# The opening of a three-layer transformer kernel: first modulation in pieces of 256 columns

## The reference, cut to what matters

```
c_act = silu(c)                                    # 1024 values
mod = c_act @ ada_w[0] + ada_b[0]                  # 1024 x 6144
sh1, sc1, g1, sh2, sc2, g2 = split(mod, 6)
h = rms_norm(x, norm_g[0, 0]) * (1 + sc1) + sh1
z = gelu(h @ a_w_in); u, v = split(z, 2)           # 1024 x 2048
v = layer_norm(v, a_ln_g, a_ln_b)
mixed = einsum(tril(a_w_s), v) + a_b_s             # per group of 128 channels, over 128 tokens
y = (u * mixed) @ a_w_out
x = x + g1 * rms_norm(y, norm_g[0, 1])
```

## Time and profile before

| | us |
|---|---|
| median of 3 runs | 1553.88 |
| the runs | 1557.81, 1553.88, 1552.71 |
| span of the profiled execution | 1551.4 |
| TensorE busy in it | 1507.1 (97%) |
| DVE / ACT / POOL busy | 1095.7 / 692.6 / 286.1 |
| chain that ended last, on TensorE | 81% |

### The profile page before, as it was taken

One profiled execution on the slowest core, in us unless ns is written; L12 is line 12 of the kernel. 1 busy time (PEld: TensorE's weight loads), 2 busy tenths in 40 slices (PEclk: granted clock), 3 DMA queues, 4 the chain that ended last, 5 costly groups with the idle time before them and its releaser, 6 DMA issues.

```text
span 1551.4 us, 20894 instructions
## 1 busy us (share of the span) xinstructions
PE 1507.1 (97%) x8187; PEld 1252.2 (81%) x8187; DVE 1095.7 (71%) x1607; ACT 692.6 (45%) x1177; POOL 286.1 (18%) x230
## 2 busy tenths in 40 slices
PE   4999999999999999989999999999999999999998
PEld 3888888888888897977788988888888988677677
DVE  6798688889989764269885785556634824799775
ACT  3433551322214544357774642313233525887651
POOL 0200013223232000058870020111100011010210
PEclk9999999999999999999999999999999999999999
DMA  9675257578584315230001164443332232211101
GB/s 332 243 265 181 82 204 246 189 248 293 184 294 161 107 34 174 77 108 2 2 2 56 56 225 160 159 144 115 132 109 83 84 109 66 92 61 55 55 1 55
DMA packets 108808, 203.35 MB, mean 131 GB/s; under 512 B 6041, under 2 KB 13478, under 8 KB 108710
## 3 DMA queue, kind: packets, MB, share of 16 engines
q1 hardware_dynamic: 108710, 202.01, 38.2%
HBM read 199.90 MB, written 2.10 MB: 130 GB/s over the span
## 4 chain that ended last, share of the span: by engine, by line
PE 81%; DVE 10%; issue 3%; DMA 2%; ACT 2%; POOL 1%; SPq 1%; DVEq 0%; POOLq 0%; ACTq 0%
PE PS L2142 47%; PE PS L2095 20%; DVE MACC L1287 3%; PE PS L2477 3%; PE PS L2504 2%; DVE WL L1253 2%; PE PS L2467 2%; PE PS L2654 1%; PE PS L2166 1%; DMA MRAW<-in_ada_w_dram 1%; POOL MROW L494 1%; DMA X<-in_x_dram 1%; PE PS L2676 1%; PE PS L2469 1%; DMA RAW<-in_ff_w_in_dram 1%
## 5 line engine op out<-in xcount | busy, mean ns | idle before, releaser
L733 ACT ACTIVATE WH<-RAW 128x2048 fp32r<-128x2048 f32 (+1 forms) x111 | 208.2, 1886 | 362.4 <-DMA RAW<-in_ff_w_in_dram 223.5
L1253 DVE TENSOR_TENSOR WL<-RAW,WH 128x2048 fp32r<-128x2048 f32 (+1 forms) x107 | 269.4, 2540 | 123.3 <-ACT WH L733 123.1
L494 POOL PARTITION_ALL_REDUCE MROW<-MACC x26 | 123.3, 4743 | 601.8 <-DVE MACC L1287 514.5
L2142 PE MATMUL PS<-WH,HIDh 128*128 128x512 f32 (+1 forms) x576 | 217.4, 377 | 0.0
L2142 PE MATMUL PS<-WH,HIDl 128*128 128x512 f32 (+1 forms) x576 | 217.3, 377 | 0.0
L2142 PE MATMUL PS<-WL,HIDh 128*128 128x512 f32 (+1 forms) x576 | 217.3, 377 | 0.0
L2142 PE MATMUL PS<-HTh,WH 128*128 128x512 f32 (+1 forms) x520 | 202.5, 389 | 0.6 <-DVE WL L1253 0.6
L2142 PE MATMUL PS<-HTl,WH 128*128 128x512 f32 (+1 forms) x520 | 202.4, 389 | 0.0
L2142 PE MATMUL PS<-HTh,WL 128*128 128x512 f32 (+1 forms) x520 | 202.3, 389 | 0.0
L1287 DVE SCALAR_TENSOR_TENSOR MACC<-MRAW,CS,MACC 128x512 f32<-128x512 f32 x168 | 126.3, 752 | 8.6 <-DMA MRAW<-in_ada_w_dram 1.1
L2095 PE MATMUL PS<-HTh,WH 128*128 128x256 f32 (+1 forms) x384 | 123.8, 322 | 4.8 <-DVE WL L1253 4.5
(11 more groups left out here) (344 smaller groups left out, 2971.8 us busy)
## 6 DMA issues: line engine op xcount, KB each, us to landing
MRAW<-in_ada_w_dram SPq DMA_DIRECT2D x44, 1024.0 KB, 7.4
RAW<-in_ff_w_in_dram SPq DMA_DIRECT2D x32, 1024.0 KB, 5.4
RAW<-in_ff_w_out_dram SPq DMA_DIRECT2D x32, 1024.0 KB, 5.1
RAW<-in_w_in_dram SPq DMA_DIRECT2D x16, 1024.0 KB, 5.3
MRAW<-in_w_ada_dram SPq DMA_DIRECT2D x12, 1024.0 KB, 8.5
RAW<-in_a_w_in_dram SPq DMA_DIRECT2D x8, 1024.0 KB, 9.7
MRAW<-in_kv_ada_w_dram SPq DMA_DIRECT2D x8, 1024.0 KB, 6.2
RAW<-in_kv_w_dram SPq DMA_DIRECT2D x6, 1024.0 KB, 5.1
```

The costliest lines, as they stand in the source:

```text
L494: pool.partition_all_reduce(MROW[:], MACC[:], P, RADD).then_inc(m_red, 1)
L733: act.activation(WH[:, wslot(u), 0:width(u)], RAW[:, u % 4, 0:width(u)], ACT.Copy).then_inc(w_hi, 1)
L1253: dve.tensor_tensor(WL[:, u % 4, 0:width(u)], RAW[:, u % 4, 0:width(u)], WH[:, wslot(u), 0:width(u)].bitcast(F32), ALU.subtract).then_inc( ...
L2142: mm = pe.matmul(po, a, b_, start=(k == 0 and i == 0), stop=(k == KT - 1 and i == len(ops) - 1), skip_group_check=len(ops) > 3)
```

## The change

- The four first sums are regrouped: piece i (0 to 3) holds scale and shift of 256 channels, that is of the pair of depths 2i and 2i + 1. Each piece comes as four loads of 128 x 4 x 256. DVE sums scale and shift in turn, each instruction waiting for the last but one (`head_acc`), and the coefficients of a pair are made at once (`head_coefs`).
- c's rows are loaded alone, ahead of all else, and turned alone; the other parameter rows are issued by ACT, the last group (PR2) by SP behind the first weights, with WSR, LNB and BS.
- The weights of the first two chunks come, and are split, in pairs of depths (half slots). TensorE works through pairs, both chunks in each (`depth`), with the transposes of x just ahead (`turn_later`); XR is gone.
- ACT writes HIDh itself, and RB; DVE keeps only the subtraction (`remainder`).
- DVE starts the sum of the next pair before it does the remainders of this one.
- TensorE does three matmuls of the identity by itself behind each of the four first turned row tiles; their result is not used.
- The mixer's weights are turned and its bias matmuls done in the last pair, through one PSUM bank in two halves.
- ACT loads the table of the root ahead of x.

The core of the diff:

```diff
-        mod(0, 2)
...
-        first_mod(0)
-        for tt in range(TT):
-            load_x(tt)
-        half_weight(a_w_in[0], D, 0)
-        sp.dma_start(WSR[:], a_w_s[0].rearrange("g t s -> t g s")).then_inc(ws_in, 16)
...
+        sp.dma_start(PR1[C_C:C_C + KT, :], c[0].rearrange("(r p) -> r p", p=P)).then_inc(c_in, 16)
+        head_columns(0)
+        for tt in range(TT):
+            if tt == 2:
+                first_weight(0, 0)
+            load_x(tt)
+        first_weight(1, 0)
+        for pair in range(1, 4):
+            head_columns(pair)
+            first_weight(0, pair)
+            first_weight(1, pair)
...
+            def head_acc(i, half):
+
+                acc = (MACC, MROW)[i % 2]
+                for k in range(4 * half, 4 * half + 4):
+                    for j in range(2):
+                        a, p = acc[:, 256 * j:256 * j + 256], 2 * (i % 2) + j
+                        src = PIECE[p][:, k, :]
...
+                            dve.wait_ge(h_acc, 16 * i + 2 * k - 1 + j)
+                            dve.scalar_tensor_tensor(out=a, in0=src, scalar=CS[:, k:k + 1], in1=a,
+                                                     op0=ALU.mult, op1=ALU.add).then_inc(h_acc, 1)
...
+            first_lo(0, 0)
+            remainder(0)
+            head_acc(1, 0)
+            remainder(1)
+            first_lo(1, 0)
+            head_acc(1, 1)
+            first_lo(0, 1)
+            head_coefs(1)
...
+            for _ in range(3):
+                pe.matmul(PS[:, 2, 0:P], IDENT[:], IDENT[:], start=True, stop=True)
...
+            if pair < 3:
+                depth(0, k + 1)
+                depth(1, k)
+                head_columns(pair + 1)
+                depth(1, k + 1, (lambda: turn_later(k + 2), None, None))
+            else:
+                depth(0, k + 1, (None, lambda: weights_turned(0), None))
+                depth(1, k, (lambda: weights_turned(1), None, lambda: bias(0)))
+                depth(1, k + 1, (None, None, lambda: bias(1)))
```

More of the change, by code:

```diff
@@ new lines, in turn, with turn_later @@
+        def turn(k, tt):
+            return pe.transpose(PS[:, HEAD_BANK[k], P * tt:P * tt + P], V[:, tt, P * k:P * k + P], IDENT[:])
+        def turn_later(k):
+            pe.wait_ge(x_ev, k)
+            if k % 2 == 0:
+                pe.wait_ge(m_post, k // 2 + 1)
+            if k == 6:
+                pe.wait_ge(cols, 2)
+            for tt in range(TT):
+                mm = turn(k, tt)
+            mm.then_inc(full, 1)
+        pe.wait_ge(ones_c, 1)
+        pe.wait_ge(cols, 1)
+        head_columns(0)
@@ L2266, in turn_x @@
+        pe.wait_ge(par1_in, 16 * 6)
+        pe.transpose(PS[:, 4, P:P + PAR1], PR1[:], IDENT[0:PAR1, 0:PAR1])
+        pe.wait_ge(par0_in, 16 * 3)
+        pe.transpose(PS[:, 5, 0:P], PR0[:], IDENT[:]).then_inc(full, 3)
+        for tt in range(TT):
+            pe.wait_ge(n_xn, tt + 1)
+            for k in range(2):
+                mm = turn(k, tt)
                 if tt == TT - 1:
                     mm.then_inc(full, 1)
-        pe.wait_ge(ones_c, 1)
-        pe.wait_ge(cols, 1)
-        column(0, MACC)
@@ new lines, in pe_program, with depth @@
+        xn[0] += TT
+        pe.wait_ge(ev_d, 2)
+        def depth(c_, k, after=(None, None, None)):
+            pair, u, o = k // 2, 2 * c_ + k // 4, 512 * (k % 4)
+            pe.wait_ge((wp_lo, w_lo)[pair % 2], 2 * (pair // 2) + c_ + 1)
+            h, l = WH[:, u, o:o + 512], WL[:, u, o:o + 512]
+            for i in range(3):
+                if c_ == 0 and i != 1:
+                    pe.wait_ge((tile_hi, None, tile_rdy)[i], k + 1)
+                for b in range(4 - c_):
+                    a = (HIDl if i == 2 else HIDh)[:, k, P * b:P * b + P]
+                    mm = pe.matmul(bank(3 + c_, b), a, l if i == 1 else h, start=(k == 0 and i == 0),
+                                   stop=(k == KT - 1 and i == 2), skip_group_check=True)
+                    if i == 2 and k == KT - 1:
+                        mm.then_inc(full, 1)
+                    elif i == 2 and b == 3 and k == 3:
+                        mm.then_inc(w_used, 1)
+                if after[i] is not None:
+                    after[i]()
@@ L2309, in pe_program, with weights_turned, bias @@
+        def weights_turned(i):
+            if i == 0:
+                pe.wait_ge(pool_c, 4)
+                pe.wait_ge(x_ev, 8)
+            else:
+                pe.wait_ge(mix_w, 1)
+            for g in range(4):
+                mm = pe.transpose(PS[:, 3, P * g:P * g + P], WSR[:, 4 * i + g, :], IDENT[:])
+            mm.then_inc(mix_t, 1)
+        def bias(i):
+            if i == 0:
                 pe.wait_ge(mix_w, 2)
                 pe.wait_ge(ln_in, 16)
-                pe.wait_ge(x_raw, 4)
@@ L2336, in pe_program @@
+        pe.wait_ge(mix_e, 2)
+        for k in range(KT):
+            mm = three(bank(4, 3), k, slice(3 * P, 4 * P), "B", HIDh, HIDl, 2 + k // 4)
+            if k == 3:
+                mm.then_inc(w_used, 1)
+        mm.then_inc(full, 1)
         n.group, n.chunk, n.tile = 5, 2, 8
         def mod_column(m, acc):
-            pe.wait_ge(m_acc, 8 * m + 8)
+            pe.wait_ge(m_acc, 8 * (m - 3))
             for b in range(4):
```

343 lines of the change are left out of this document (151 added, 192 removed).

## The result

The changed kernel takes 1565.34 us (median of 4 runs, 1562.88 to 1565.98), the kernel before 1553.3 in the same job; the ratio is 1.0064, 95% interval 1.0046 to 1.0083. The forecast was 1556.4 us, with a range up to 1563. The profiled execution's span is 1563.0 us against 1551.4.

A forecast was written before the change was run, and what follows sets the result against it. TensorE, busy almost throughout from 83.17 us, was taken as the bound. Its 7.1 us lead against 9.6 of waits gave +2.5 us, on the median 1553.88 a forecast of 1556.4 us; range 1553.5 to 1559, widened to 1550 to 1563.

The forecast's parts named there:

- The start: Opening: x complete about 16 to 16.9 us, first projection matmul at 21.1 (20.3 to 21.4), ten us earlier than before.
- Fillers: Opening, filling matmuls on TensorE: nothing counted for them; if they do nothing, under 1 us, inside the forecast; no chance given.
- DVE's pieces of 256: Opening column sums on DVE: 0.405 us per 256-column instruction, bounds 0.38 and 0.53; a pass takes 6.2 us.
- rival 2: Opening slower: DVE's instructions dearer (1562 us); also 1 KB rows under 280 GB/s (+3), slow reduce set-up; chance 0.33 together.
- TensorE to the last bias: Opening: 46.0 us of work plus 3.0 of waits from 21.1; last bias matmul 70.1, last MIXC copy 70.7.
- GpSimd, "add and reduce 6.5 to 8.4, I take 7.5": Behind MIXC's copies at 70.7: add then reduce take 7.5 us, GATE written at 79.6, 3.5 later than before.
- port rule: DVE and GpSimd take a shared port pair in turn; add, split and reduce line up as 7.7 us.
- The chain behind GATE: From GATE to MCOL: DVE alone in unchanged order, 31.5 us long; TensorE's train shifts +2.5 us.
- The waits: TensorE behind the opening: waits 5.3 us for WL of u = 5, 3.3 for sum 6, 1.0 for MCOL; 9.6 together.
- Past that the shift stays: Rest of the kernel: later TensorE waits neither absorb nor add, so the +2.5 us shift stays to the end.
- Rival 1 (lead kept): Faster: if add and reduce were not last, MCOL at 102.3, TensorE 6.3 us earlier, 1547.6 us; chance 0.12.

The follow-up runs named there:

- e8: The changed kernel without the twelve filling matmuls of the opening; 1564.7 us, ratio 1.0061 to the kernel before.
- e12: The changed kernel with 8 overwritten matmuls at each of TensorE's three stops near 1357, 1394 and 1430 us; 1562.52 us, ratio 1.0045 to the kernel before.
- e1: The changed kernel with GpSimd reducing sums 4 and 5 first and adding BS to MIXC behind them; 1559.09 us, ratio 1.0025 to the kernel before.
- e2: As e1, and ACT rounds the weights of u = 4 ahead of the two MIXC copies; 1559.07 us, ratio 1.002 to the kernel before.
- e5: The kernel of e2 with BS added by 8 TensorE identity matmuls and no add on GpSimd; 1556.15 us, ratio 1.0002 to the kernel before.
- e3: The changed kernel with an unused one-column all-reduce on GpSimd ahead of the MIXC add; 1561.71 us, ratio 1.0052 to the kernel before.
- e4: The kernel before with a small GpSimd memset, waiting for sum 4, between the MIXC add and the reduce; 1561.35 us, ratio 1.0039 to the kernel before.
- e9: The kernel before with 8 overwritten matmuls at each of TensorE's three stops near 1357, 1394 and 1430 us; 1554.18 us, ratio 0.999 to the kernel before.
- e11: As e9, plus an unused one-column GpSimd TENSOR_TENSOR behind the last feed-forward modulation reduce near 492 us; 1553.0 us, ratio 0.9983 to the kernel before.
- e10: The kernel of e5 with DVE's and TensorE's work behind the opening reordered, plus the late edits of e11; 1550.95 us, ratio 0.9969 to the kernel before.

## Why the prediction was wrong, step by step

- **The start**: right. First scaled x at 20.49 us, first projection matmul at 21.41 (forecast 21.1).
- **Fillers**: right, nothing (e8).
- **DVE's pieces of 256**: right. Eight take 3.25 us, 0.406 each; rival 2's first half is out. So is its second: with the 1 KB rows the queue moved 344 to 384 GB/s in every window of 2 us from 22 to 40 us, not under 280.

```profile
27.22 3.25 DVE L1385 SCALAR_TENSOR_TENSOR MROW<-PIECE,CS,MROW 128x256 f32<-128x256 f32 x8
```

- **TensorE to the last bias**: the waits for DVE were 1.4 us, not 3.0, yet the last MIXC copy ended at 71.74, 1.0 later than forecast; the matmuls, transposes and column sums between took 71.1 - 21.4 - 1.4 = 48.3 us where my sum of pieces has 46.0.
- **GpSimd, "add and reduce 6.5 to 8.4, I take 7.5"**: this is the step that failed. The MIXC copy's end to the reduce's end took 83.10 - 71.74 = 11.4 us: add 2.40, gap 5.63, reduce 3.25. Add and reduce alone, 5.65, are even less than I took; the port rule's blocking did not meet them, since DVE's split (2.80 instead of 2.29) was held and not the add. The gap has no term in the sum. I named it ("a reduce that is slow to set up right behind an ordinary POOL instruction; in before 15 us of idle hid any such cost") and left it without a price inside another rival. The trace of before had the nearest prices: 8.56 and 7.80 us of "issue" at 669 and 1258 us, where GpSimd goes the other way, from the reduces to a TENSOR_TENSOR and an IOTA; and it had the MODIFY_POOL_CONFIG right behind the add. The way that mattered, from the add to the reduce, stands there only with idle time over it. With 5.6 in the sum the forecast is 1556.4 + 5.6 - 1.8 + 1.0 = 1561.2 us. The median is 4.1 us above that; in the profiled execution falls of the granted clock add 4.7, and 0.9 comes back (below). The port rule in the prediction put 2.3 + 2.3 + 3.2 us in a row; the gap pulled the three apart.
- **The chain behind GATE**: right, 31.5 us again. With GATE 4.95 later than forecast the shift of TensorE's train is 2.5 + 4.95 = 7.45 us; measured 7.7.
- **The waits**: places right, sizes not: 9.0, 1.4 and 0.6 where 5.3, 3.3 and 1.0 were forecast. They sum to 11.0 against 9.6; a longer first wait takes from the later ones.
- **"Past that the shift stays"**: wrong in both directions by small amounts: 0.9 came back between 320 and 470 us, and 3 falls of the granted clock brought 4.7 in the profiled execution. e12 against the changed kernel puts the falls in the stops at 2.8 us of the median (different jobs). The runs of the kernel before spread with the clock as well; whether the changed one gets more falls by its timing or by chance of four runs is open. Their mean clocks can't be compared as they stand, since the slow restart at 90 to 110 us (0.54 and 0.94) alone takes 0.003 off the changed kernel's.
- **Rival 1 (lead kept)**: its condition, reduces not behind the bias, was made in e1, e2 and e5, and the lead was still not kept. Its price, 1547.6, leaves out the reduce itself, which GATE waits for. In e5, which has no add on GpSimd at all, sum 4 starts at 63.84 us, the reduce runs from 70.03 to 75.20, and GATE is written at 76.66, no earlier than the 76.10 of before. It also leaves out the slow restart of a TensorE that gets ahead of DVE, and in e1 and e2 the add's weight on DVE. So the changed opening without the gap and without the add is even with the kernel before (e5: ratio 1.0002), not faster.

## What to carry to other kernels

Before an instruction is moved later, ask what the idle time behind it was hiding, and look through the whole trace for "issue" gaps of that engine at changes of instruction kind: they carry a price. Look at the engine's queue too: an instruction that the timeline leaves out can stand there. An engine's lead is worth something only if the chain it next waits for gets shorter too; shorten that chain first, then start earlier. Where TensorE must wait some 2 us, a few matmuls into a place that is overwritten anyway cost nothing at the three stops tried here, and the spread of the runs was narrower; in the opening they gave nothing (e8).

## What the runs showed of the hardware

- GpSimd: from TENSOR_TENSOR to the all-reduce 5.6 to 6.2 us without an instruction on its timeline (changed, e3, e8, e12), 7.55 behind a memset (e4); from the all-reduce to TENSOR_TENSOR 8.4 to 9.0 us (before, changed, e1 to e9, e11, e12) and 6.9 in e10. A MODIFY_POOL_CONFIG stands at its start. It is hidden only by idle time behind the last instruction ahead of it. MEMSET, AFFINE_SELECT and CAST behind the reduces (656.96 to 660.8 us in before) start without such a gap.
- DVE and GpSimd: where an add or a reduce overlapped a split, the one that started second was held, with one exception below. Add 3.27 beside a split, 2.40 where it started first; a DVE instruction of 0.48 took 2.63 beside the add (e2). The Trainium skill ("SBUF — State Buffer", section "Who interferes with whom") calls the shared ports an exclusive lock. The rows of the add agree. Those of the reduce agree when it starts second (5.17 beside a split, 3.23 alone), but not for its whole length when it starts first: the split of the earlier trace rows began with 1.8 us of the reduce left and took 2.94 us instead of 2.29, 0.65 more and not 1.8. The rows of before, changed and e4 fit ports that come free 2.1 us into a reduce of 3.23, and a split that starts 2.25 us into one takes its plain 2.29 (e1, at 88.08). Here the measurement decides.
- TensorE: after waits of 2.3 to 9 us the restart ran partly at the lower of its two levels (1.2 GHz; the lowest window of 10 us behind them had a granted clock of 0.52 to 0.83 in the changed kernel and in e1 to e5); a column sum and mix of 4.47 us took 7.35 in e1. After stops of 2.2 us it did so in 11 of 20 cases, for 1.6 us each, and after stops of 1.5 us in none of 10.
